# The last norm and the store of y: a final norm in rows of tokens, made of products with diagonals of the gain

## What is computed

```python
        x = x + g2[:, None, :] * f
    return rmsnorm(x, final_norm_g), ...

def rmsnorm(x, g):
    xf = x.astype(jnp.float32)
    y = xf * lax.rsqrt(jnp.mean(xf * xf, axis=-1, keepdims=True) + EPS)
    return (y * g.astype(jnp.float32)).astype(x.dtype)
```

## Time and profile before

| | us |
|---|---|
| median of three executions | 1809.38 |
| the profiled execution | 1811.69 |
| its span on the core | 1809.9 |
| PE busy in the span | 1638.7 |
| DVE busy | 753.3 |
| ACT busy | 369.7 |
| POOL busy | 100.1 |
| first instruction of the last norm (L567) to the end of the span | 22.1 |

### The profile page before, as it was taken

How to read it: one execution, slowest core, us unless ns; L and a number is a source line. 1 busy time by engine, 2 the same in 40 slices (tenths; PEclk the granted TensorE clock), 3 DMA queues, 4 the chain that set the end, 5 groups by cost and what they waited for, 6 DMA issues and landing times. The chain is left out here.

```text
span 1809.9 us, 29578 instructions
## 1 busy us (share of the span) xinstructions
PE 1638.7 (91%) x11504; PEld 1097.5 (61%) x11504; DVE 753.3 (42%) x1784; ACT 369.7 (20%) x790; POOL 100.1 (6%) x122
## 2 busy tenths in 40 slices
PE   7998899988999999999996987788999999999996
PEld 4786665856565655656563766566565655556563
DVE  2204436127535344443535113546545453444535
ACT  2011443021212121111212223321111121211111
POOL 0000010000000000000000000000000000000000
PEclk9999999989999999999998988899999999999998
DMA  9994698339999999999997592536999999999980
GB/s 369 385 365 141 240 393 330 105 131 398 375 416 417 415 418 415 417 412 415 412 395 267 219 342 87 204 123 245 391 417 416 416 418 414 417 412 414 414 342 25
DMA packets 173695, 603.95 MB, mean 334 GB/s; under 512 B 18382, under 2 KB 67698, under 8 KB 138683
## 3 DMA queue, kind: packets, MB, share of 16 engines
q1 hardware_dynamic: 156874, 559.89, 78.6%
q0 software_dynamic: 16128, 40.92, 6.0%
q10 hardware_dynamic: 624, 2.23, 0.3%
HBM read 594.42 MB, written 26.90 MB: 343 GB/s over the span
## 5 line engine op out<-in xcount | busy, mean ns | idle before, releaser
L2089 PE MATMUL ps<-ring,scratch 128*64 128x256 f32 x4352 | 481.9, 380 | 31.9 <-DMA ring<-in_moe_w_up 30.0
L2089 PEld LDWEIGHTS ps<-ring,scratch 128*64 128x64 f32 x4352 | 331.6, 137 | 169.2 <-issue 42.8
L2121 PE MATMUL ps<-ring,scratch 128*64 128x512 f32 x1088 | 243.5, 599 | 1.7 <-ACT scratch L2481 1.7
L2070 PE MATMUL ps<-scratch 128*128 128x264 bf16 x1632 | 195.5, 277 | 5.7 <-issue 5.7
L2384 DVE SCALAR_TENSOR_TENSOR scratch<-scratch,ps 128x256 f32<-128x256 f32 x68 | 32.6, 481 | 391.7 <-ACT scratch L2473 391.6
L717 PE MATMUL ps<-hT,ring 128*128 128x264 f32 x768 | 185.1, 399 | 1.3 <-ACT hT L359 1.3
L2070 PEld LDWEIGHTS ps<-scratch 128*128 128x128 bf16 x1632 | 141.5, 97 | 64.2 <-issue 19.7
L717 PEld LDWEIGHTS ps<-hT,ring 128*128 128x128 f32 x768 | 150.7, 197 | 30.8 <-issue 1.6
L2121 PEld LDWEIGHTS ps<-ring,scratch 128*64 128x64 f32 x1088 | 69.7, 136 | 147.9 <-issue 101.1
L2365 DVE TENSOR_TENSOR scratch<-scratch,ps 128x264 f32<-128x264 f32 x272 | 116.7, 429 | 64.8 <-PE ps L2070 64.8
L2473 ACT ACTIVATE scratch<-ps 128x256 f32<-128x256 f32 x68 | 26.2, 385 | 484.8 <-PE ps L2089 484.8
(11 more groups left out here) (331 smaller groups left out, 1353.5 us busy)
## 6 DMA issues: line engine op xcount, KB each, us to landing
ring<-in_moe_w_gate SPq DMA_DIRECT2D x136, 1024.0 KB, 19.1
ring<-in_moe_w_up SPq DMA_DIRECT2D x136, 1024.0 KB, 19.0
ring<-in_moe_w_down SPq DMA_DIRECT2D x136, 1024.0 KB, 17.0
ring<-in_ada_w SPq DMA_DIRECT2D x48, 1024.0 KB, 12.2
ring<-in_ret_w_in SPq DMA_DIRECT2D x24, 1024.0 KB, 15.7
ring<-in_state_ret SPq DMA_DIRECT2D x16, 1024.0 KB, 15.1
out_ret_sample<-ring POOLq DMA_DIRECT2D x16, 1024.0 KB, 8.8
ring<-in_gla_w_in SPq DMA_DIRECT2D x12, 1024.0 KB, 8.0
```

Source lines behind the costliest of these rows:

```text
L2070: mm = nc.tensor.matmul(k.ps[:, c % 2, 0:T], row_parts[:, p, s, c * P:(c + 1) * P], slot_token[:, p, :], start=(p == 0 and s == 0), stop=( ...
L2089: mm = nc.tensor.matmul(k.ps[lo:lo + CAP, 2 + p, j * DE:(j + 1) * DE], xg[:, p, c, lo:lo + CAP], slot(k, n, DE)[:, c, :], start=(c == 0), ...
L2121: mm = nc.tensor.matmul(k.ps[lo:lo + CAP, 6 + half, :], hid_t[:, p, m, lo:lo + CAP], slot(k, n, D)[:, m, half * 512:(half + 1) * 512], sta ...
```

## The change

`final` no longer calls `norm`; it is one block.

- POOL builds eight diagonal matrices, the identity times the gain of each of the 128 features of a chunk, in `k.ring`.
- DVE adds the experts' output as before.
- ACT squares the chunks as before, now into `k.ring`.
- PE multiplies, per chunk, the three token groups of `k.x` (as weights) with the chunk's diagonal (as the moving operand of 128 columns). That gives x times gain in rows of tokens, in the PSUM places where the transposes went. Then it multiplies the squares of the two prompt groups (as weights) with one column of ones, accumulating in one column each of banks 6 and 7; the samples' eight such products follow behind the last chunk.
- The sum of squares is then one value per token on the partition of the token. Mean, root and reciprocal are pairs of instructions on 2 columns for the prompt and 1 column for the samples.
- DVE scales and copies the first 512 columns of each group, ACT the other 512, both to `y`, now in `k.ring`.
- SP stores each half by itself: six DMAs in the order DVE's half, ACT's half, for each group.

```diff
--- before.py
+++ after.py
@@ -1766,33 +1766,87 @@
 
 
 def final(k):
+
     nc, out = k.nc, k.out
-    norm(k, DEPTH, 0)
-    s_tr, s_cp, s_st = k.sem("y_token_major"), k.sem("y_copied"), k.sem("y_stored")
-    y = k.scratch[:, 0:TT * D].rearrange("p (t d) -> p t d", t=TT)
+    sc = k.scratch
+    acc, x_gate, x_small = k.pending
+    k.pending = None
+    s_d, s_xn, s_sq, s_pr, s_sum, s_ms, s_rt, s_sc, s_st = (k.sem(f"final_{n}") for n in (
+        "gains_placed", "experts_added", "squared", "token_major", "summed", "meansq", "root", "scaled", "stored"))
+    c_ya, c_yv = k.sem("final_y_scalar"), k.sem("final_y_vector")
+    diagonal = k.ring[:, 0:D].rearrange("p (c n) -> p c n", c=DC)
+    y = k.ring[:, D:D + TT * D].rearrange("p (t d) -> p t d", t=TT)
+    squares = k.ring[:, SLOT * 2:SLOT * 2 + DC * T].rearrange("p (c t) -> p c t", c=DC)
+    small = k.rstd[:, 0:3 * TT].rearrange("p (i t) -> p i t", i=3)
     with nc.Block() as block:
+        @block.gpsimd
+        def _(pool):
+            for c in range(DC):
+                nc.gpsimd.tensor_scalar(diagonal[:, c, :], k.ident, k.fin_g[:, c:c + 1], None, ALU.mult)\
+                    .then_inc(s_d, 1)
+
+        @block.vector
+        def _(v):
+            link = lambda ins: k.dve.link(v, ins)
+            link(nc.vector.tensor_tensor(x_small, acc[:, :, TP:T], x_gate[:, :, 1:NCOND], ALU.mult))
+            nc.vector.tensor_tensor(k.x[:, :, TP:T], x_small, k.x[:, :, TP:T], ALU.add).then_inc(s_xn, 1)
+            for c in range(DC):
+                nc.vector.scalar_tensor_tensor(k.x[:, c, 0:TP], acc[:, c, 0:TP], x_gate[:, c, 0:1], k.x[:, c, 0:TP],
+                                               ALU.mult, ALU.add).then_inc(s_xn, 1)
+            v.wait_ge(s_sum, 1)
+            nc.vector.tensor_scalar(small[:, 0, 0:2], k.ps[:, 6:8, 0:1].rearrange("p b n -> p (b n)"), 1.0 / D, EPS,
+                                    ALU.mult, ALU.add)
+            nc.vector.tensor_scalar(small[0:NS, 0, 2:3], k.ps[0:NS, 6, 1:2], 1.0 / D, EPS, ALU.mult, ALU.add)\
+                .then_inc(s_ms, 1)
+            v.wait_ge(s_rt, 1)
+            nc.vector.reciprocal(small[:, 2, 0:2], small[:, 1, 0:2])
+            nc.vector.reciprocal(small[0:NS, 2, 2:3], small[0:NS, 1, 2:3]).then_inc(s_sc, 1)
+            v.wait_ge(s_sc, 1)
+            for t, (_, n) in enumerate(TOKENS):
+                nc.vector.tensor_scalar(y[0:n, t, 0:512], k.ps[0:n, 2 * t, :], small[0:n, 2, t:t + 1], None,
+                                        ALU.mult).then_inc(c_yv, 1)
+
+        @block.scalar
+        def _(act):
+            for c in range(DC):
+                act.wait_ge(s_xn, c + 2)
+                nc.scalar.activation(squares[:, c, :], k.x[:, c, :], ACT.Square).then_inc(s_sq, 1)
+            act.wait_ge(s_ms, 1)
+            nc.scalar.activation(small[:, 1, 0:2], small[:, 0, 0:2], ACT.Sqrt)
+            nc.scalar.activation(small[0:NS, 1, 2:3], small[0:NS, 0, 2:3], ACT.Sqrt).then_inc(s_rt, 1)
+            act.wait_ge(s_sc, 1)
+            act.wait_ge(s_pr, DC)
+            for t, (_, n) in enumerate(TOKENS):
+                nc.scalar.activation(y[0:n, t, 512:D], k.ps[0:n, 2 * t + 1, :], ACT.Copy, scale=small[0:n, 2, t:t + 1])\
+                    .then_inc(c_ya, 1)
+
         @block.tensor
         def _(pe):
-            for t, (t0, n) in enumerate(TOKENS):
-                for c in range(DC):
-                    mm = nc.tensor.transpose(k.ps[0:n, 2 * t + c // 4, (c % 4) * P:(c % 4 + 1) * P],
-                                             k.h[:, c, t0:t0 + n], k.ident)
-                mm.then_inc(s_tr, 1)
-
-        @block.vector
-        def _(v):
-            for t, (_, n) in enumerate(TOKENS):
-                v.wait_ge(s_tr, t + 1)
-                nc.vector.tensor_copy(y[0:n, t, :], k.ps[0:n, 2 * t:2 * t + 2, :].rearrange("p b d -> p (b d)"))\
-                    .then_inc(s_cp, 1)
+            for c in range(DC):
+                pe.wait_ge(s_d, c + 1)
+                pe.wait_ge(s_xn, c + 2)
+                for t, (t0, n) in enumerate(TOKENS):
+                    mm = nc.tensor.matmul(k.ps[0:n, 2 * t + c // 4, (c % 4) * P:(c % 4 + 1) * P], k.x[:, c, t0:t0 + n],
+                                          diagonal[:, c, :], start=True, stop=True)
+                mm.then_inc(s_pr, 1)
+                pe.wait_ge(s_sq, c + 1)
+                for t in range(2):
+                    nc.tensor.matmul(k.ps[:, 6 + t, 0:1], squares[:, c, t * P:(t + 1) * P], k.ones[:, 0:1],
+                                     start=(c == 0), stop=(c == DC - 1))
+            for c in range(DC):
+                mm = nc.tensor.matmul(k.ps[0:NS, 6, 1:2], squares[:, c, TP:T], k.ones[:, 0:1], start=(c == 0),
+                                      stop=(c == DC - 1))
+            mm.then_inc(s_sum, 1)
 
         @block.sync
         def _(sp):
             for t, (t0, n) in enumerate(TOKENS):
-                sp.wait_ge(s_cp, t + 1)
                 dst = out["y_prompt"][0, t0:t0 + n] if t < 2 else out["y_sample"].rearrange("b o d -> (b o) d")
-                sp.dma_start(dst, y[0:n, t, :]).then_inc(s_st, 16)
-            sp.wait_ge(s_st, 16 * TT)
+                sp.wait_ge(c_yv, t + 1)
+                sp.dma_start(dst[:, 0:512], y[0:n, t, 0:512]).then_inc(s_st, 16)
+                sp.wait_ge(c_ya, t + 1)
+                sp.dma_start(dst[:, 512:D], y[0:n, t, 512:D]).then_inc(s_st, 16)
+            sp.wait_ge(s_st, 2 * 16 * TT)
```

## The result

| | median of the runs, us | ratio to before, 95% interval | profiled execution, us | its span |
|---|---|---|---|---|
| before | 1811.88 (12 runs) | | 1811.69 | 1809.9 |
| after | 1819.16 (12 runs) | 1.0040, 1.0030 to 1.0049 | 1821.47 | 1819.6 |

The forecast was 1805.7 us, with a range up to 1811.0. The changed kernel is slower, by 7.3 us between the medians of 12 runs each (1819.16 - 1811.88). By the bound of the prediction (0.5%) that still is "within"; the sign is wrong all the same, since the interval lies wholly above 1, and the time lies outside the range. Of the 13.5 us between forecast and median, 2.5 are no fault of the reckoning: it started from the median of three executions of before, 1809.38, and that of 12 is 1811.88, which is already above the range. The other 11.0 are a change of +7.3 where -3.7 was forecast.

A forecast was written before the change was run, and what follows sets the result against it. The kernel's end was taken as a chain with one engine working at a time: sums ready +5.0, then -7.7 to the first store's issue, stores -1.0, so 3.7 us off 1809.38 gives 1805.7 us, range 1802.5 to 1811.0.

The forecast's parts named there:

- PE stretch: PE from its first product at 1788.7 to the samples' last sum at 1799.6, taken as 10.9 us.
- first issue to end: From the first store's issue to the end of the span: 4.6 us, against 5.6 before.
- With the clock rising at 1792.3 as before: TensorE's clock goes from 1.2 to 2.4 GHz at 1792.3, with 2.1 chunks done; the other 5.9 take 6.5 us.
- case A: Rival: PE's clock does not rise, eight chunks take 13.8 us, the gain is gone, 1809.4 us; chance 0.13.
- three quarters of a chunk's time are ordinary products: Argument that PE's clock rises: most of a chunk is 128-column products like those after which it rose before.
- I take 0.22 at either clock: Price in us of one one-column float32 product on PE, with 0.10 and 0.43 as ends.
- the lower row: Earlier trace of PE: 128-column float32 weights with nine columns moving, eight records in 1.05 us, 0.13 a record at most.
- case B: Rival: low clock and float32 weights bound PE, one-column products 0.43, a chunk 2.15, 1813.6 us; chance 0.04.
- the 1.0 us: Gain expected at the stores, from first issue to end: 5.6 us down to 4.6.
- Case E: Rival: half-row stores move slower or six issues queue, the end comes at 1806.7 to 1807.7; chance 0.06.
- the small steps: Mean, root and reciprocal between PE's sums and the scaling, on 2 columns and 1: 0.95 us.
- the point of balance: The kernel gets slower once PE needs more than 14.6 us from first product to last sum.

The follow-up runs named there:

- wide_ones: After with the prompt's sum products moving 128 columns of ones instead of one, same weights; 1812.44 us, ratio to before 1.0008.
- sums_last: After with PE's order changed: all 24 products with the diagonals first, then the one-column sums; 1811.18 us, ratio to before 1.0000.
- whole_rows: After with one store for each token group, three DMAs instead of six; 1819.16 us in one run.
- wide_grouped: After with 128 columns of ones in the sum products and the samples' diagonal products behind all chunks; 1809.67 us, ratio to before 0.9982.
- turned: Against before: PE only transposes x, ACT squares and sums the turned rows, DVE scales by root and gain; 1803.90 us, ratio 0.9944.

## Why the prediction was wrong

Step by step, forecast against measured, in us of tail:

| step | forecast | measured |
|---|---|---|
| PE's first product after the block's start | 0.9 | 1.1 |
| PE stretch | 10.9 | 20.9 |
| last sum to first issue | 2.0 | 1.6 |
| first issue to end | 4.6 | 5.5 |
| change of the tail | -3.7 | +7.0 |

The differences add up: -3.7 + 0.2 + 10.0 - 0.4 + 0.9 = +7.0. Ten of the 10.7 are PE's.

**The step that failed is "With the clock rising at 1792.3 as before".** In after it fell just before PE's first product (0.69 in the mean of the window from 1791) and stayed at 0.50 to the end. I had put case A, that it does not rise, at 0.13, with "three quarters of a chunk's time are ordinary products" against it. That count was made with one-column products at 0.22; at 1.2 GHz they take 0.43, and in the real chunk the ordinary products of 1.28 us are half of 2.53. In wide_ones, with the same products and 128 columns moving in each, the clock rose; in sums_last it rose in the wide products and fell in the one-column ones. PE was busy in all of these stretches. By the forecast's own terms the clock alone is worth 3.7 us, as case A had it: 8 x 1.73 + 0.8 = 14.6 instead of 10.9.

**The second is the price of a one-column product.** "I take 0.22 at either clock" joined two rows that don't meet: the earlier trace rows bounded the load at each clock, and the lower row, 0.13 a record, was read without its clock. The granted clock was 1.00 there (the window 7.00:7.50 of before), so it bounds a product at 2.4 GHz, 0.26, and says nothing against 0.43 at 1.2 GHz, for which case B used it. It is 0.22 at 2.4 GHz and 0.43 at 1.2, the ends that the earlier trace rows gave, each for its clock: 16 x 0.21 = 3.4 us. The two errors go together: the one-column products come with the low clock (sums_last), and the low clock doubles their price. The prediction gave the low clock with cheap loads 0.13 and with dear ones 0.04 (case B); by the earlier trace rows and these runs the dear ones belong to the low clock.

**A term was missing from the sum**, the switches between 128- and 8-column weights: 0.39 us a chunk, 3.1 in all, which no case had. So the chunk took 2.53 where case B had 2.15, and the time of 1813.6 that B gave is 5.6 below the median, of which 2.5 are the starting point. The rest of the 10 us is the samples' sums, the other way: 16 records in 0.55 us, 0.07 a product where 0.10 was taken.

**The stores did not get the 1.0 us** of the sum, a gain that no row showed. Case E had named the loss, but for another reason, that half rows or six issues are slow: from the first issue to the end the 1.08 MB take 5.55 us before and 5.54 after, and whole_rows, with three stores, still takes 5.31.

**Right were:** the start of PE; the diagonals off the path at 0.60 to 0.84 us each (0.52 taken, 1.04 the end); the small steps (0.83 from DVE's first instruction to the scaling, forecast 0.95; the way from the last sum to DVE took 0.03, forecast 0.3); both halves (0.69 and 0.61) side by side; and, nearly, the point of balance, "more than 14.6 us from its first product to the last sum": wide_ones has 14.8 and a ratio of 1.0008, wide_grouped 11.2 and 0.9982, after 20.9 and 1.0040. By the tails it lies lower, at about 13.9 (22.1 less 1.1, 1.6 and 5.5), since the stores gained nothing.

Against the transposes the prediction weighed a rule of the Trainium skill (TensorE: Matmul & The Clock Gate, Part 4), that they do not count as PE activity. The trace of turned doesn't bear it out: with transposes alone on PE from 1790.75 to 1795.25 the clock is at 0.89 in the mean of the window from 1794 and 1.00 in the next.

```profile
1793.00:1794.00 1.00, 1.00 (x7) 1.00 (x6) 0.47 (x2) 1.00 (x4) 0.00 (x0) 0.50 0.01 4
1794.00:1795.00 1.00, 1.00 (x10) 0.74 (x8) 0.00 (x0) 0.64 (x4) 0.00 (x0) 0.89 0.00 0
1795.00:1796.00 1.00, 0.25 (x3) 0.00 (x0) 0.26 (x2) 0.68 (x4) 0.00 (x0) 1.00 0.00 0
```

Before's own transposes don't bear it out either. The 0.50 at 1805 on which case A leaned is not the whole of them: they last until 1806.34, and the next window has 0.96 in the mean, so that the clock rose at about 1806.1, while they still ran.

```profile
1806.00:1807.00 1.00, 0.34 (x3) 0.00 (x0) 0.64 (x2) 0.00 (x0) 0.00 (x0) 0.96 0.61 246
```

**Open:** why the clock rises 3.7 us after the first product in wide_grouped and 6.5 after it in wide_ones and in sums_last; how few one-column products already keep the clock down, since no chunk had fewer than two; and what PE does in the 0.2 us of a change of width.

## What to carry to other kernels

Price a float32 product by its weight columns as well as its moving columns, at the granted clock: with 128-column weights and one column moving it costs as much as with 128 moving, so a sum over the partitions with the data as weights is no cheap add-on. Where the gain hangs on the clock rising, don't take the rise from PE being busy; look whether the new list has one-column products between the wide ones, and price the low clock and the long loads as one case. And before products are added to save a chain of small steps, look for an engine that can do the sum in an instruction it needs anyway: ACT's square with a sum, on rows of tokens, left PE only the 24 transposes, 4.5 us where after's stretch is 20.9.

## What the runs showed of the hardware

- A float32 product with 128-column weights costs 0.43 us at 1.2 GHz and 0.22 at 2.4 with one moving column as with 128; with 8-column weights and one column it costs 0.07 at 1.2 GHz (eight in 0.55).
- PE can be busy for 20 us without a gap and be granted 1.2 GHz throughout; widening the moving operand of its one-column products to 128 columns lets it rise and shortens the tail by 6.1 us (ratio to before 1.0040 and 1.0008).
- Changing between 128- and 8-column weights costs about 0.2 us a time at 1.2 GHz (0.39 for two) and about 0.14 at 2.4 (a chunk of 1.40 less ten records of 0.112, for two).
- Float32 transposes alone let the clock rise: in turned at about 1794.2, 3.5 us after they began, and in before at about 1806.1, 5.0 us after.
- A diagonal of 128 by 128 float32 takes POOL 0.84 us beside DVE's additions and 0.60 without them.
